# The last two down-projection units taken in two passes over token halves, and roots spread through stride-zero weights

## The reference, cut to what matters

```python
def rms_norm_2(x, g):
    x32 = x.astype(jnp.float32)
    y = x32 * lax.rsqrt(jnp.mean(x32 * x32, axis=-1, keepdims=True) + RMS_EPS)
    return (y * g.astype(jnp.float32)).astype(x.dtype)
...
        h = rms_norm_2(x, g_ffn[l])
        up = depthwise_conv(h @ w_up[l], conv_f_w[l], conv_f_b[l], FFN_CONV // 2)
        act = jax.nn.gelu(up[..., :D_FF_2], approximate=True) * up[..., D_FF_2:]
        x = x + act @ w_down[l]
    return rms_norm_2(x, g_final)
```

## Time and profile before

| | us |
|---|---|
| median of 3 runs (lowest, highest) | 1883.85 (1882.17, 1885.89) |
| the profiled execution's own time | 1883.64 |
| its span, first to last instruction | 1881.9 |
| PE busy in it | 1855.5 |
| DVE busy in it | 1243.5 |
| ACT busy, POOL busy | 523.6, 15.4 |

### The profile page before, as it was taken

One profiled execution on the slowest core, in us unless ns is written; L12 is line 12 of the kernel. 1 busy time (PEld: TensorE's weight loads), 2 busy tenths in 40 slices (PEclk: granted clock), 3 DMA queues, 4 the chain that ended last, 5 costly groups with the idle time before them and its releaser, 6 DMA issues.

```text
span 1881.9 us, 21566 instructions
## 1 busy us (share of the span) xinstructions
PE 1855.5 (99%) x8620; PEld 1482.7 (79%) x8620; DVE 1243.5 (66%) x1670; ACT 523.6 (28%) x481; POOL 15.4 (1%) x57
## 2 busy tenths in 40 slices
PE   8999999999999999999999999999999999999997
PEld 6888888878888778888888888877778888788875
DVE  6763667667745487443244779979975788726874
ACT  5333222122322222221122112148852122212210
POOL 0000000000000000000000000000000000000000
PEclk9999999999999999999999999999999999999998
DMA  5224341472111332222322224232224222232221
GB/s 203 89 82 153 111 157 64 149 263 99 68 68 46 112 134 76 103 84 84 122 90 72 84 90 157 90 112 85 76 70 162 90 90 98 75 104 103 81 72 71
DMA packets 48132, 194.64 MB, mean 103 GB/s; under 512 B 6720, under 2 KB 15296, under 8 KB 33344
## 3 DMA queue, kind: packets, MB, share of 16 engines
q1 hardware_dynamic: 48064, 193.70, 29.9%
HBM read 180.84 MB, written 12.85 MB: 103 GB/s over the span
## 4 chain that ended last, share of the span: by engine, by line
PE 77%; issue 20%; DVE 3%; DMA 0%; ACT 0%; POOLq 0%; POOL 0%; SPq 0%; DVEq 0%
PE bank L942 23%; PE bank L943 23%; PE bank L944 23%; PE xb L1217 2%; DVE wlo L1292 1%; PE xb L1163 0%; PE xb L1153 0%; PE bank L1059 0%; PE bank L1060 0%; PE bank L1061 0%; PE xb L1171 0%; PE xb L981 0%; PE xb L1120 0%; PE xb L974 0%; DVE x L1336 0%
## 5 line engine op out<-in xcount | busy, mean ns | idle before, releaser
L942 PE MATMUL bank<-uhi,whi 128*128 128x512 f32 x1552 | 622.9, 401 | 7.2 <-DVE wlo L2138 7.0
L943 PE MATMUL bank<-ulo,whi 128*128 128x512 f32 x1552 | 616.7, 397 | 0.0
L944 PE MATMUL bank<-uhi,wlo 128*128 128x512 f32 x1552 | 616.6, 397 | 0.0
L654 ACT ACTIVATE whi<-raw 128x2048 fp32r<-128x2048 f32 (+3 forms) x177 | 299.9, 1694 | 1101.8 <-PE bank L944 1073.1
L1292 DVE TENSOR_TENSOR wlo<-raw,whi 128x2048 fp32r<-128x2048 f32 (+3 forms) x177 | 356.5, 2014 | 80.3 <-ACT whi L654 77.9
L942 PEld LDWEIGHTS bank<-uhi,whi 128*128 128x128 f32 x1552 | 293.3, 189 | 80.2 <-issue 9.7
L944 PEld LDWEIGHTS bank<-uhi,wlo 128*128 128x128 f32 x1552 | 293.3, 189 | 71.6
L943 PEld LDWEIGHTS bank<-ulo,whi 128*128 128x128 f32 x1552 | 293.6, 189 | 71.0 <-issue 1.4
L942 PE MATMUL bank<-hhi,whi 128*128 128x512 f32 x528 | 209.8, 397 | 2.3 <-DVE hlo L1345 1.2
L943 PE MATMUL bank<-hlo,whi 128*128 128x512 f32 x528 | 209.3, 396 | 0.0
L944 PE MATMUL bank<-hhi,wlo 128*128 128x512 f32 x528 | 209.3, 396 | 0.0
(11 more groups left out here) (391 smaller groups left out, 1815.4 us busy)
## 6 DMA issues: line engine op xcount, KB each, us to landing
raw<-in_up SPq DMA_DIRECT2D x65, 1024.0 KB, 4.8
raw<-in_win SPq DMA_DIRECT2D x16, 1024.0 KB, 4.8
raw<-in_wout SPq DMA_DIRECT2D x8, 1024.0 KB, 4.9
raw<-in_down1a SPq DMA_DIRECT2D x8, 768.0 KB, 4.4
tab<-tab_kept SPq DMA_DIRECT2D x4, 1536.0 KB, 8.6
raw<-in_down2a SPq DMA_DIRECT2D x8, 768.0 KB, 4.4
raw<-in_down3a SPq DMA_DIRECT2D x8, 768.0 KB, 4.3
raw<-in_down1b SPq DMA_DIRECT2D x8, 640.0 KB, 4.0
```

The source lines that it names most:

```text
L654: act.activation(whi[s][:, 0:width], raw[s][:, 0:width], ACT.Copy).then_inc(w_hi, 1)
L942: pe.matmul(dst, wh, hi, start=first, stop=False)
L943: pe.matmul(dst, wh, lo, start=False, stop=False)
L944: return pe.matmul(dst, wl, hi, start=False, stop=last)
```

## The change

Two things are changed.

1. *Roots are spread without diagonals, everywhere.* PE takes the column of roots itself, read 128 times with a stride of zero, as weights, and the identity as the moving operand (`root_columns`). DVE's diagonals go, with DVE's wait for POOL; PE now waits for POOL's semaphore `rs_ready` directly. In the second mixer DVE forms the product of the two roots, signals `roots_made`, and PE makes both spreads before k = 1 of the second unit (`spread_two`).
2. *The last two down units and the last norm go by halves of the tokens* (`last_pair`). PE multiplies unit m = 6 and then m = 7 for tokens 0 to 255, then both again for tokens 256 to 511, with matmuls of 256 columns. Half a root's sums are made of `acc` (the first seven squares) and, separately, of `sq` (the eighth), and are added by DVE (`part_means`, `half_root`). The first half's sums and spread, and the second half's sums over `acc`, stand between matmuls; the second half's sums over `sq` and its spread stand behind the last one. DVE scales the first half of the eight tiles in two lots, six before the last residual and two behind it. SP stores two tiles of one token half at a time.

The diff, without semaphore declarations, the same edit of the first mixer's `o_spread` (L1131) and `states` (L1949), and the calls at the end of DVE's program:

```diff
             ffn(nb, A["up3"], (A["down3a"], A["down3b"]))
-            for k in range(KD):
-                sp.wait_ge(out_ready, k + 1)
-                sp.dma_start(out[k * P:(k + 1) * P, :], x[:, k, :]).then_inc(stored, 16)
+            for t in range(2):
+                tok = slice(t * S // 2, (t + 1) * S // 2)
+                for k in range(0, KD, 2):
+                    sp.wait_ge(out_ready, KD * t + k + 2)
+                    sp.dma_start(out[k * P:(k + 2) * P, tok].rearrange("(m p) s -> p m s", p=P), x[:, k:k + 2, tok])\
+                        .then_inc(stored, 16)
...
-            def inverse_root(width=4):
+            def inverse_root(width=4, at=0):
                 pool.wait_ge(rt_ready, norms.step())
-                pool.tensor_tensor(out=nstat[:, 0:width], in0=nstat[:, 0:width], in1=nstat[:, 8:8 + width],
-                                   op=ALU.pow).then_inc(rs_ready, 1)
+                pool.tensor_tensor(out=nstat[:, at:at + width], in0=nstat[:, at:at + width],
+                                   in1=nstat[:, 8:8 + width], op=ALU.pow).then_inc(rs_ready, 1)
...
             inverse_root()
-            inverse_root()
+            inverse_root(2, 0)
+            inverse_root(2, 2)
...
-            def spread_roots(to=1):
-                pe.wait_ge(diag_ready, ndiag.step())
-                for c in range(4):
-                    last = pe.matmul(XB[to][:, c * P:(c + 1) * P], ones[:, :], diag[:, c, :],
+            def root_columns(to, at, width=4):
+                for c in range(width):
+                    last = pe.matmul(XB[to][:, c * P:(c + 1) * P],
+                                     nstat[:, at + c:at + c + 1].broadcast_to([P, P]), ident[:, :],
                                      start=True, stop=True)
-                last.then_inc(spread, 1)
+                return last
+            def spread_roots():
+                pe.wait_ge(rs_ready, n_root.step())
+                root_columns(1, 0).then_inc(spread, 1)
+            def spread_two():
+                pe.wait_ge(rs_ready, n_root.step())
+                pe.wait_ge(roots_made, 1)
+                root_columns(1, 4).then_inc(spread, 1)
+                root_columns(2, 0).then_inc(spread, 1)
...
-            def ffn(nb, rooted=rooted, between_down={}):
+            def last_pair(nb, tiles):
+                for t in range(2):
+                    tok = slice(t * S // 2, (t + 1) * S // 2)
+                    for j in range(2):
+                        s = (nb + j) % 2
+                        if t == 0:
+                            pe.wait_ge(w_lo, nb + j + 1)
+                            pe.wait_ge(evac[s], (nb + j) // 2)
+                        for k in range(tiles):
+                            if t == j == 1 and k == 1:
+                                half_spread(0)
+                            if j and k == 6:
+                                half_sums(t, acc, acc_ready, nacc)
+                            if t and j == 0 and k == 4:
+                                half_sums(0, sq, last_sq, n_sq)
+                            last = product(DB[s][t][:, 0:S // 2], (whi[s], wlo[s]), slice(k * P, (k + 1) * P),
+                                           hhi[:, k, tok], hlo[:, k, tok], k == 0, k == tiles - 1)
+                        last.then_inc(tail_out, 1)
+                half_sums(1, sq, last_sq, n_sq)
+                half_spread(1)
+            n_sq = Tally(last_sq)
+            def half_sums(t, src, ready, tally):
+                pe.wait_ge(ready, tally.step())
+                for c in range(2 * t, 2 * t + 2):
+                    at = c if src is acc else 4 + c
+                    last = pe.matmul(XB[2 * t][:, at:at + 1], src[:, c * P:(c + 1) * P], ones[:, 0:1],
+                                     start=True, stop=True)
+                last.then_inc(sums_out, 1)
+            def half_spread(t):
+                pe.wait_ge(rs_ready, n_root.step())
+                for c in range(2 * t, 2 * t + 2):
+                    last = pe.matmul(XB[2 * t + 1][:, c * P:(c + 1) * P],
+                                     nstat[:, c:c + 1].broadcast_to([P, P]), ident[:, :], start=True, stop=True)
+                last.then_inc(spread, 1)
+            def ffn(nb, rooted=rooted, between_down={}, ends=False):
...
                     nb += tiles
-                    rolled(pe, KD // 2, down_turn, [])
+                    if ends and h == 1:
+                        rolled(pe, KD // 2 - 1, down_turn, [])
+                        last_pair(nb + KD - 2, tiles)
+                    else:
+                        rolled(pe, KD // 2, down_turn, [])
...
                 between[0] = {5: [lambda: sum_squares((acc, acc_2))]}
-                between[1] = {1: [spread_roots], 5: [lambda: spread_roots(2)]}
+                between[1] = {1: [spread_two]}
...
             nb += FFN_UNITS + M2_UNITS
-            ffn(nb)
-            sum_squares()
-            spread_roots()
+            ffn(nb, ends=True)
...
             n_norm = Tally(sums_out)
-            n_rs = Tally(rs_ready)
             n_spread = Tally(spread)
             def means(sums, over):
                 dve.wait_ge(sums_out, n_norm.step())
                 dve.tensor_scalar(nstat[:, 0:4], sums, 1.0 / over, EPS, ALU.mult, ALU.add).then_inc(rt_ready, 1)
-                dve.wait_ge(rs_ready, n_rs.step())
             def root():
                 dve.engine_nop().then_inc(acc_ready, 1)
                 means(XB[0][:, 0:4], D)
-                diagonals(0)
                 dve.wait_ge(spread, n_spread.step())
-            def diagonals(at):
-                for c in range(4):
-                    last = dve.tensor_scalar(diag[:, c, :], ident[:, :], nstat[:, at + c:at + c + 1], None, ALU.mult)
-                last.then_inc(diag_ready, 1)
...
                     nb -= KD
-                    down_turn(KD // 2 - 1, following)
+                    if ends and h == 1:
+                        last_pair(nb + KD - 2)
+                    else:
+                        down_turn(KD // 2 - 1, following)
                     nb += KD
+            def last_pair(nb):
+                tt, ts, stt = dve.tensor_tensor, dve.tensor_scalar, dve.scalar_tensor_tensor
+                def add_in(t, j):
+                    m, tok = KD - 2 + j, slice(t * S // 2, (t + 1) * S // 2)
+                    dve.wait_ge(tail_out, 2 * t + j + 1)
+                    then(tt(out=x[:, m, tok], in0=DB[(nb + j) % 2][t][:, 0:S // 2], in1=x[:, m, tok], op=ALU.add))
+                    square = tt(out=sq[:, tok], in0=x[:, m, tok], in1=x[:, m, tok], op=ALU.mult)
+                    if j:
+                        square.then_inc(last_sq, 1)
+                    else:
+                        then(square)
+                        tt(out=acc[:, tok], in0=acc[:, tok], in1=sq[:, tok], op=ALU.add).then_inc(acc_ready, 1)
+                def part_means(t):
+                    dve.wait_ge(sums_out, n_norm.step())
+                    ts(nstat[:, 4 + 2 * t:6 + 2 * t], XB[2 * t][:, 2 * t:2 * t + 2], 1.0 / D, EPS, ALU.mult, ALU.add)
+                def half_root(t):
+                    dve.wait_ge(sums_out, n_norm.step())
+                    stt(out=nstat[:, 2 * t:2 * t + 2], in0=XB[2 * t][:, 4 + 2 * t:6 + 2 * t], scalar=1.0 / D,
+                        in1=nstat[:, 4 + 2 * t:6 + 2 * t], op0=ALU.mult, op1=ALU.add).then_inc(rt_ready, 1)
+                def scaled(t, ms):
+                    tok = slice(t * S // 2, (t + 1) * S // 2)
+                    for m in ms:
+                        stt(out=x[:, m, tok], in0=x[:, m, tok], scalar=col("g_final_2", m), in1=XB[2 * t + 1][:, tok],
+                            op0=ALU.mult, op1=ALU.mult).then_inc(out_ready, 1)
+                add_in(0, 0)
+                part_means(0)
+                add_in(0, 1)
+                half_root(0)
+                add_in(1, 0)
+                dve.wait_ge(spread, n_spread.step())
+                scaled(0, range(6))
+                part_means(1)
+                add_in(1, 1)
+                scaled(0, range(6, KD))
+                half_root(1)
+                dve.wait_ge(spread, n_spread.step())
+                scaled(1, range(KD))
...
                     ts(nstat[:, 4:8], nstat[:, 4:8], EPS, None, ALU.add).then_inc(rt_ready, 1)
-                    dve.wait_ge(rs_ready, n_rs.step())
-                    then(tt(out=nstat[:, 4:8], in0=nstat[:, 0:4], in1=nstat[:, 4:8], op=ALU.mult))
-                    diagonals(4)
+                    dve.wait_ge(rs_ready, 1 + 1 + PAIRS + 1 + 1)
+                    tt(out=nstat[:, 4:8], in0=nstat[:, 0:4], in1=nstat[:, 4:8], op=ALU.mult).then_inc(roots_made, 1)
                     dve.wait_ge(spread, n_spread.step())
                     keep_inverse(inv_late)
-                    diagonals(0)
```

More of the change, by code:

```diff
@@ L1131, in o_spread @@
                 def o_spread(p):
-                    pe.wait_ge(diag_ready, ndiag.step())
-                    for h in range(4):
```

(5 more changed lines are left out.)

12 lines of the change are left out of this document (5 added, 7 removed).

## The result

The changed kernel takes 1877.38 us, the median of five runs (1876.73 to 1878.90), against 1883.85 (1882.17 to 1885.89, the three runs shown above and two more) before: a ratio of 0.9967, 95% interval 0.9956 to 0.9978. The profiled execution has a span of 1877.2 us, against 1881.9.

The account below looks back on a forecast made before the run. TensorE's matmul stream was taken to bound the kernel, with a 16.55 us tail behind it. Stream +2.50 and shorter tail links summed to 3.6 us less, 1883.85 to 1880.2 us; range 1877.9 to 1882.4.

Parts of the forecast that it names:

- The stream: TensorE's last two units: smaller matmuls add 0.46 us and four in-stream jobs 2.04, so the last matmul starts 2.50 later.
- The first job: First half-width sums inside TensorE's last two units, waiting for VectorE's chain: 0.6 us, against 0.48 for each other job.
- The cover for unit 7's weights: VectorE's weight split for the last unit ends 0.6 us before TensorE needs it, so no wait.
- POOL's power: GpSimd's root in the last norm's tail: 0.09 us hand-over and 1.01 us, as before.
- sums: Tail after the last matmul: sums to root's input 0.99 us, counting 0.2 us by which two first-half scalings outlast their cover.
- Store and close: End of the kernel: 3.0 us becomes 3.0 to 3.3 with shorter rows of 1 KB; 3.07 taken.
- The scalings: VectorE's eight half-width scalings in the tail: 0.48 us plus seven steps of 0.39, 3.21 us, 2.15 less than before.
- The roots elsewhere: All other norms: 44 diagonals fall away, 9.6 us of VectorE, costed at nothing; bound up to 1.6 us gain.
- Rival 4: All spreads: stride-zero reading slows weight loads, 0.47 us a pass instead of 0.12, 31 us more, time 1911; chance 0.04.
- Rival 3: Second half-token pass cramped: VectorE or unit 7's weights late, TensorE waits mid-stream; gain 1 to 2 us, 1882.3; chance 0.09.
- Rival 1: Hand-overs dearer: spread at half clock, stream jobs at upper bound, slower store; gain 2.1 to 3.1 us, 1881.2; chance 0.21.
- I subtract from the median: Step from terms to time: the 3.6 us gain is taken from the median 1883.85, giving 1880.2.

Follow-up runs that it names:

- the last version: Kernel after with acc and acc_2 sums separated, first-half sums one k later, ScalarE applying gain early to six tiles: 1876.67 us (6 runs), ratio 0.9967 to kernel before.
- the power at four columns: Kernel after, but POOL's last power takes four columns instead of two: 1881.08 us in one run.
- all ahead: Kernel after, but all eight scalings of the first half stand before the last residual: 1878.82 us in one run.
- Before again: The kernel before, measured again without an edit: 1883.78 us (11 runs), ratio 0.9996 to the kernel before.
- roots only: Kernel before with only the new spread of roots, last two units and last norm left whole: 1882.94 us (11 runs), ratio 0.9993 to kernel before.
- after again: The kernel after, measured again without an edit: 1879.17 us (9 runs), ratio 0.9974 to the kernel before.
- single stores: Kernel after, but the second half is stored tile by tile, eight DMAs of 128 KB: 1877.74 us in one run.
- sums apart: Kernel after, but in the second mixer sums of acc stand before k=6 and of acc_2 before k=7: 1877.03 us (5 runs), ratio 0.9963 to kernel before.

## Why the prediction was right in direction and wrong in size

**The stream** was forecast to be 2.50 us longer and is 2.40. Its steps cost 14.09/119 = 0.118 us each (0.120 forecast, -0.19 in all). The first job, from the start of the matmul before it (1857.03) to 1858.06, cost 1.03 - 0.24 = 0.79 (0.6 forecast), 0.34 more than the others, since it had to wait for the chain of DVE; one k later, in the last version, it did not. The three others cost 0.44 to 0.45 (0.48). That price had been rounded down, as 1.07 us for eight passes of the sums is 0.13 each and not 0.11 to 0.12, and it came out lower still. The cover for unit 7's weights held: PE has no wait there. PE's own weight loads rose by 68 to 8688, the 60 extra matmuls among them, and hid under the matmuls.

**The tail** by the links of the prediction:

| link | forecast | measured |
|---|---|---|
| last start to DVE | 0.39 | 0.32 |
| residual, square | 0.88 | 0.88 |
| to PE, sums, root's input | 0.10 + 0.99 | 0.06 + 0.80 |
| POOL | 0.09 + 1.01 | 0.08 + 0.70 |
| hand-over, spread | 0.05 + 0.61 | 0.05 + 0.75 |
| eight scalings | 3.21 | 3.22 |
| store and close | 3.07 | 2.66 |

The end piece was thus forecast 3.64 us shorter and is 4.62. Three terms were mis-sized on the dear side. **POOL's power** was put in "as before"; it has half the columns, which was overlooked: 0.31 us, shown by the power at four columns. The **sums** were charged 0.2 us for two scalings; all ahead shows these to be hidden: 0.19 us. **Store and close** was raised by 0.07 for the shorter rows and fell by 0.3 from the 2.99 us before: 0.41 us. The last DMA is waited for as long as before, and the closing round behind it is shorter. SP's waits of the kernel before, then of after, are:

```profile
SPq L160 <- DMA out_xT<-x: 1.9, 1, 1.9
SPq L160 <- PEq L160: 0.5, 1, 0.5
```

```profile
SPq L160 <- DMA out_xT<-x: 1.9, 1, 1.9
SPq L160 <- PEq L160: 0.2, 1, 0.2
```

Before again and roots only have the 0.5, every kernel with halves has 0.2; why is open. Against these goes the half spread, which needs 0.75 us to DVE's start, not 0.61. The rest of the difference is small: 0.10 in the stream, 0.11 in the first links.

**The scalings** came out to 0.01 us. The Trainium skill's rule on the fixed cost of each instruction ("VectorE: DVE Perf Modes", section on the TRN2 errata) is borne out in kind: of a half scaling's step of 0.39 us 0.12 is fixed, where the page's some 150 cycles are 0.156. Its advice for tiles of 512 elements and more did not hold for this tail: the price was paid for the first half beside PE's stream, and only eight half steps were left exposed.

**The roots elsewhere** cost and gained nothing, as forecast. The loads of stride zero take what the ordinary ones of the earlier trace rows take. The kernel after, line 987, ns min/median/max:

```profile
L987 PEld LDWEIGHTS xb<-ident,nstat x80: 185/190/192, 28.4 to 1505.0; 128*128 128x128 f32 x80
```

Rival 4 falls with that. Rival 3 falls with the last residual, which starts 0.32 us after its matmul with DVE idle for 0.67 us before it; of its signs only the small delay of the first job came. Rival 1 was right in one of its parts: the spread ran at full clock in six of the ten profiles with halves, and at half clock in the other four. That the result's profile had the full clock, as forecast, was luck. The prediction's reason, that the clock had stayed full for 3.7 us behind the stream before, does not carry: in after again it fell 2.2 us behind the last matmul's start, with the spread at 2.89. The other outcome costs 0.5 us.

**The steps that failed** are two, and it took both to leave the range.

The first is the sum of the new tail: POOL's power "as before", the two scalings "I count it", and the store at 3.07 us. It gave 3.6 us where the end piece gained 4.6. With every term right, the forecast would have been 1883.85 - 4.6 = 1879.2, inside the range, and larger samples gave 1879.17 and 1878.62.

The second, and the larger, is the step from the terms to the time: "I subtract from the median". The remaining 1.9 us are not a gain of the change. Executions of either kernel also differ by the two falls of the clock, at 1.5 us each, and by up to 1.7 us at the start. The five spans after were 1875.0, 1875.2, 1875.6, 1877.0 and 1877.2 us; the last is the profiled one with one fall, and three lie 1.6 to 2.2 us below it, about one fall. That these three had no fall is argued from their spans and granted clocks (0.999 against 0.998), as their traces were not kept; single stores is a trace without a fall, at a span of 1876.0. That the median of five came from this group was luck of the draw.

The prediction had read one of these falls in the earlier trace rows, at the right price, but made its absence part of a rival, with 0.11 for that and a wait of PE together. It should have been a spread around every case: zero, one or two falls. Its range ended at 1877.9 for that; the right terms without one fall give 1877.7. So the direction and the mechanism of the gain were right, and the number was not.

## What to carry to other kernels

Work that stands behind the last matmul is worth halving even at the price of more and smaller matmuls: here 2.4 us of stream bought 7.0 us of tail (0.5 less where the clock falls before the spread). Before an operation is put down as unchanged, look at its width; and read its price per column from the other widths in the trace. Where five executions decide a difference of some us, look how many of them the larger sample would put at the edge. Where the trace shows the clock fall inside a busy stream, treat it as something that executions have or have not, and put its price on both ends of the range.

## What was not expected of the hardware

- The granted clock falls to half for 3.4 us inside a stream in which PE is 99% busy, and costs 1.5 us each time. It happened at two places only: one behind a wait of 0.3 us and 16 one-column passes, one behind waits of 1.2 and 0.4 us. It fell there in some executions and not in others of the same kernel. The Trainium skill ("TensorE: Matmul & The Clock Gate", the table of states) gives the half clock to an idle array; here PE had idled for 0.3 us at the first site, and for 1.2 and 0.4 us at the second. The cause is not shown.
- POOL's power over 128 partitions takes 0.70, 1.01 and 1.64 us for 2, 4 and 8 columns in the kernel after, 0.157 us a column.
- From the start of the last matmul of the stream the clock stayed full for 5.3 us in the kernel after and for 2.2 us in sums apart and in after again, with like work behind it.
- In single stores SP needs 0.47 us to issue a store of 128 KB in rows of 1 KB, one behind the other.
